# A hybrid decoder trunk on TensorE: gate on 80 partitions, paired levels, a diagonal on VectorE

## What is computed

```python
def rmsnorm(x, g):
    return x * rsqrt(mean(x * x, axis=-1) + EPS) * g

def hybrid_mixer(h, cos, sin, w_in, w_a2, b_a2, ret_norm_g, gla_norm_g, w_out):   # h = rmsnorm(x, mix_pre_g)
    rq, rk, rv, rg, gq, gk, gv, ga, gg = split(h @ w_in)     # ga has 16 columns, gq and gk 256 each
    ro = retention(rope(rq), rope(rk) * 64 ** -0.5, rv)      # chunks of 128 tokens, 4 heads
    ro = rmsnorm(ro, ret_norm_g) * silu(rg)
    log_a = log_sigmoid(ga @ w_a2 + b_a2) / 16               # 16 -> 256, per key dimension
    go = gla(gq * 64 ** -0.5, gk, gv, log_a)                 # gated linear attention, 4 heads
    go = rmsnorm(go, gla_norm_g) * silu(gg)
    return concat(ro, go) @ w_out

# gla, unchunked: S_t = diag(exp(log_a_t)) S_{t-1} + k_t^T v_t ;  o_t = q_t S_t
# so the score of query i on key j <= i is sum_d q_id k_jd exp(cum_id - cum_jd), cum the running sum of log_a;
# for i = j the exponent is 0 and the score is q_i . k_i
```

## Time and profile before

| | us |
|---|---|
| median of 3 runs | 1191.17 (1190.92 to 1191.26) |
| profiled execution | 1191.56 |
| its span, first to last instruction | 1189.8 |
| TensorE busy | 1182.7 |
| VectorE busy | 831.0 |
| ScalarE busy | 703.1 |
| GpSimd busy | 147.7 |

### The profile page before, as it was taken

How to read it: one execution, slowest core, us unless ns; L and a number is a source line. 1 busy time by engine, 2 the same in 40 slices (tenths; PEclk the granted TensorE clock), 3 DMA queues, 4 the chain that set the end, 5 groups by cost and what they waited for, 6 DMA issues and landing times. The chain is left out here.

```text
span 1189.8 us, 17467 instructions
## 1 busy us (share of the span) xinstructions
PE 1182.7 (99%) x6224; PEld 1001.9 (84%) x6224; DVE 831.0 (70%) x1290; ACT 703.1 (59%) x1223; POOL 147.7 (12%) x230
## 2 busy tenths in 40 slices
PE   9999999999999999999999999999999999999998
PEld 8888888778888888888888888887888888888886
DVE  6866546788767678775487875477887676777752
ACT  7655446756666557654476664376566665666641
POOL 3000002473100100000000000026531001000000
PEclk9999999999999999999999999999999999999999
DMA  9755555354545365556465555554445444555540
GB/s 366 258 183 195 198 207 185 136 213 142 168 169 177 116 209 191 193 195 211 142 213 199 189 198 191 194 207 136 171 142 183 153 163 155 191 202 180 196 173 36
DMA packets 33350, 217.81 MB, mean 183 GB/s; under 512 B 3953, under 2 KB 4209, under 8 KB 9729
## 3 DMA queue, kind: packets, MB, share of 16 engines
q1 hardware_dynamic: 33136, 216.77, 52.6%
q10 hardware_dynamic: 144, 0.13, 0.0%
HBM read 215.84 MB, written 1.05 MB: 182 GB/s over the span
## 5 line engine op out<-in xcount | busy, mean ns | idle before, releaser
L1539 DVE SCALAR_TENSOR_TENSOR w_lo<-raw,first,w_hi 128x512 fp32r<-128x512 f32 x576 | 414.7, 774 | 87.9 <-ACT w_hi L1084 87.4
L1084 ACT ACTIVATE w_hi<-raw,first 128x512 fp32r<-128x512 f32 x568 | 368.7, 715 | 98.9 <-PE acc L756 47.5
L755 PE MATMUL acc<-xT,w_hi 128*128 128x512 f32 x864 | 300.2, 391 | 0.0
L756 PE MATMUL acc<-xT,w_lo 128*128 128x256 f32 x864 | 241.9, 280 | 0.0
L580 PE MATMUL acc<-w_hi,xT 128*128 128x512 f32 x576 | 228.7, 397 | 0.0
L581 PE MATMUL acc<-w_hi,xT 128*128 128x512 f32 x576 | 224.6, 390 | 0.0
L584 PE MATMUL acc<-w_lo,xT 128*128 128x512 f32 x576 | 224.4, 390 | 0.0
L755 PEld LDWEIGHTS acc<-xT,w_hi 128*128 128x128 f32 x864 | 161.6, 187 | 35.4
L1531 DVE TENSOR_TENSOR w_lo<-raw,w_hi 128x1024 fp32r<-128x1024 f32 x112 | 124.6, 1146 | 89.9 <-ACT w_hi L1078 89.6
L756 PEld LDWEIGHTS acc<-xT,w_lo 128*128 128x128 f32 x864 | 163.3, 189 | 0.1
L1078 ACT ACTIVATE w_hi<-raw 128x1024 fp32r<-128x1024 f32 x112 | 106.6, 991 | 95.3 <-PE acc L584 78.7
(11 more groups left out here) (224 smaller groups left out, 1382.7 us busy)
## 6 DMA issues: line engine op xcount, KB each, us to landing
raw<-in_gu SPq DMA_DIRECT2D x86, 1024.0 KB, 5.1
raw<-in_down SPq DMA_DIRECT2D x32, 1024.0 KB, 4.8
raw<-in_in SPq DMA_DIRECT2D x24, 1024.0 KB, 5.1
raw<-in_kv SPq DMA_DIRECT2D x16, 1024.0 KB, 5.1
raw<-in_down SPq DMA_DIRECT2D x16, 768.0 KB, 4.2
raw<-in_out SPq DMA_DIRECT2D x8, 1024.0 KB, 5.1
raw<-in_q SPq DMA_DIRECT2D x8, 1024.0 KB, 5.1
raw<-in_o SPq DMA_DIRECT2D x8, 1024.0 KB, 5.0
```

What stands on the lines that cost most here:

```text
L755: pe.matmul(o[:, :], w_hi[:, slot, kk, c:c + P], xT[:, :, k, :], start=k == 0, stop=False)
L756: mm = pe.matmul(o[:, TOK:2 * TOK], w_lo[:, slot, kk, c:c + P], xT_hi[:, k, :], start=False, stop=k == KD - 1)
L1084: act.activation(w_hi[:, slot, k, :], raw[:, slot, k, :], ACT.Copy, scale=gains[:, ds(g, 1)]).then_inc(s_hi, 1)
L1539: dve.scalar_tensor_tensor(w_lo[:, slot, k, :], raw[:, slot, k, :], gains[:, ds(g, 1)], w_hi[:, slot, k, :].bitcast(F32), ALU.mult, ALU.su ...
```

## The change

The mixer's input is normalised before it is transposed, as for the FFNs. The low-rank gate's weights stand five times side by side in 80 columns (hi, lo, hi, hi, hi), so that ga comes out on 80 partitions, and 16 matmuls (all 80 columns times xT_hi, then times xT_lo) replace 24. VectorE rounds the 80 rows to fp32r and puts the remainder into rows 32 to 47; w_a2 stands on the same 80 partitions (three times, zeros, once more, of which its low part is kept), so that one fp32r product per half gives the logits. The diagonal comes from VectorE: query times key, row sums, times the identity. Two levels share one use of the banks, each with its half (`LV_USE`, `LV_HALF`); the second retention keys share with level 0. The squares of `mem` and its 1/rms move into the down chunks of the first FFN.

```diff
-M_USES = ["z", "diag", "rj0", "rj1", "lv0", ..., "lv7", "ro", "go", "s0", "s1"]
+M_USES = ["z", "rj0", "rj1lv0", "lv1", "lv23", "lv45", "lv67", "ro", "go", "s0", "s1"]
+LV_USE = ["rj1lv0", "lv1", "lv23", "lv23", "lv45", "lv45", "lv67", "lv67"]
+LV_HALF = [1, 0, 0, 1, 0, 1, 0, 1]
 # SyncE: mem is loaded in layer 0's first FFN, mem_t behind the mixer's last x transposes
+                if (l, f) == (0, 0):
+                    sp.wait_ge(s_tev, 4)
+                    sp.dma_start(mem_t[:, :, :], a["mem"].rearrange("(t p) d -> p t d", p=P)).then_inc(s_mem, 16)
-                        sp.wait_ge(s_x, l * 16 + 8)
+                        sp.wait_ge(s_t, t_no(l, ("x", 1, 1, 1)) + 1)
-                            sp.wait_ge(s_msq, 2)
 # TensorE
-                norm = phase in (0, 3, 4)
+                norm = phase != 2
+                    if d == 3 and (l, f) == (0, 0):
+                        pe.wait_ge(s_rmem, TT)
+                        for i in range(TT):
+                            mm = pe.matmul(mb[0][:, i * P:(i + 1) * P], r_mem[:, i:i + 1].to_broadcast([P, P]),
+                                           ident[:, :], start=True, stop=True)
-                late = (dict(before_last=lambda: x_transposes(l, 1, 0)) if f == 0 else
-                        dict(mids={3: lambda: x_transposes(l, phase + 1, 0)}))
+                     ..., mids={3: lambda: x_transposes(l, phase + 1, 0)})
                     for kt in range(KD):
-                        three(mb[0][0:RANK, 0:TOK], w_ga_hi[:, kt, :], w_ga_lo[:, kt, :], xT_hi[:, kt, :],
-                              xT_lo[:, kt, :], kt == 0, kt == KD - 1)
-                    pe.wait_ge(s_rpre, l * 8 + 2 + 1 + 1)
-                    for t in range(TT):
-                        mm = pe.matmul(mb[0][0:RANK, TOK + t * P:TOK + (t + 1) * P],
-                                       r_pre[:, t:t + 1].to_broadcast([P, RANK]), ident[:, :], start=True, stop=True)
+                        st = w_ga_cols[:, kt, :, :].rearrange("p c r -> p (c r)")
+                        pe.matmul(mb[0][0:GA_COLS, 0:TOK], st, xT_hi[:, kt, :], start=kt == 0, stop=False)
+                        mm = pe.matmul(mb[0][0:GA_COLS, 0:TOK], st, xT_lo[:, kt, :], start=False, stop=kt == KD - 1)
-                inside = {4: {4: diagonal}, 5: {4: lambda: retention_scores(0)}, 6: {4: lambda: level(l, 0)}, ...
+                def second_keys():
+                    retention_scores(1)
+                    level(l, 0, False, True)
+                inside = {5: {4: lambda: retention_scores(0)},
+                          6: {4: lambda: level(l, 1, True, True)}, 10: {4: retention_outputs}}
+                behind = {4: rqk_transposes, 5: second_keys, 6: lambda: levels(l, 2), 7: lambda: levels(l, 4),
+                          8: lambda: levels(l, 6), 10: gated_outputs, 11: lambda: mixed_transposes(l, 0)}
 # ScalarE, start of the mixer (boundary() now has the FFNs' order too)
+                x_square(l, 1, 1)
                 act.wait_ge(s_gas, l + 1)
-                act.activation(w_ga_hi[:, :, :], w_ga_s[:, :, :], ACT.Copy).then_inc(s_gah, 1)
+                act.activation(w_ga_cols[:, :, :, :], w_ga_s[:, :, :].unsqueeze(2).to_broadcast([P, KD, 5, RANK]),
+                               ACT.Copy).then_inc(s_gah, 1)
+                act.activation(w_a2_l[:, :], w_a2[:, l, :], ACT.Copy).then_inc(s_a2hi, 1)
                 split_hi(l, C_IN + 1, 1)
                 x_hi(l, 1, 1)
-                x_square(l, 1, 1)
-                act.wait_ge(s_rpre, l * 8 + 2 + 0 + 1)
-                project(0, 0, gqk[:, 0, :], r_pre)
+                project(0, 0, gqk[:, 0, :], 1.0)
 # VectorE
+                x_norm(l, 1, 1)
                 dve.tensor_tensor(w_ga_s[:, :, :], ..., g_mix, ALU.mult).then_inc(s_gas, 1)
                 split_lo(l, C_IN + 1, 1)
                 x_lo(l, 1, 1)
-                dve.tensor_copy(r_row, mb[0][0:RANK, TOK:2 * TOK]).then_inc(s_rrow, 1)
-                dve.tensor_tensor(gaT, mb[0][0:RANK, 0:TOK], r_row, ALU.mult).then_inc(s_mf[0], 1)
+                dve.tensor_copy(gaT[:, :], mb[0][0:GA_COLS, 0:TOK]).then_inc(s_gahi, 1)
+                low = slice(2 * RANK, 3 * RANK)
+                dve.tensor_tensor(gaT[low, :], mb[0][low, 0:TOK], gaT[low, :].bitcast(F32),
+                                  ALU.subtract).then_inc(s_mf[0], 1)
+                dve.tensor_tensor(qk, gqk[:, :, 0:256], gqk[:, :, 256:512], ALU.mult).then_inc(s_qk, 1)
+                dve.tensor_reduce(qk_dot[:, :], pr0[:, 0]..., AX.X, ALU.add).then_inc(s_qk, 1)
                 for e in range(2):
-                    dve.tensor_tensor(pg[:, e], mb[e][:, :].rearrange("p (c i) -> p c i", c=4),
-                                      ident[:, :].unsqueeze(1).to_broadcast([P, 4, P]), ALU.mult).then_inc(s_mf[e], 1)
+                    dve.tensor_tensor(pg[:, e], ident[:, :].unsqueeze(1).to_broadcast([P, 4, P]), d,
+                                      ALU.mult).then_inc(s_pg, 1)
                 retention_mask(1)
-                split_lo(l, C_IN + 4, 0, ks=(0, 1))
                 level_out(0)
-                split_lo(l, C_IN + 4, 0, ks=(2, 3))
-                split_lo(l, C_IN + 4, 1, ks=(0, 1))
+                split_lo(l, C_IN + 4, 0)
                 level_out(1)
```

More of the change, by code:

```diff
@@ L807, in level @@
                 A = av[n % 2].rearrange("p (r i) -> p r i", r=2)
-                for e in range(2):
-                    wait_m(l, f"lv{n}", e)
-                if l == 0 and n == 6:
-                    pe.wait_ge(s_rmem, TT)
-                    for t in range(TT):
-                        pe.matmul(mb[0][:, TOK + t * P:TOK + (t + 1) * P], r_mem[:, t:t + 1].to_broadcast([P, P]),
-                                  ident[:, :], start=True, stop=True)
+                c0 = LV_HALF[n] * TOK
+                if first:
+                    for e in range(2):
+                        wait_m(l, LV_USE[n], e)
                 if b == P:
@@ L819, in level @@
                             rows = slice(64 * e, 64 * e + 64)
[L820 removed]
+                            mm = pe.matmul(mb[e][:, c0 + r * P:c0 + (r + 1) * P], A[rows, r, 0:P], A[rows, r, P:2 * P],
                                            start=True, stop=True)
[L822 removed]
+                            if last and r == 1:
                                 mm.then_inc(s_m[e], 1)
@@ L2246, in _ @@
                     pool.wait_ge(s_const, 16 * 5)
+                    for t in range(TT):
+                        mem_norm(l, t)
                 post(l, 0, 0)
```

231 lines of the change are left out of this document (113 added, 118 removed).

## The result

The changed kernel takes 1193.77 us (median of 15 runs, 1193.32 to 1194.88), the kernel before 1191.17 beside it: 1.0021 times as long, 95% interval 1.0014 to 1.0028. The forecast was 1188.4, and the time lies above its range. The profiled execution took 1193.32 us, 1.76 more than that of before.

The account below looks back on a forecast made before the run. TensorE, busy 1182.7 of 1189.8 us, was taken as the bound. Program −8.8, boundary +4.9 and middle +1.2 make −2.7: 1188.9 us profiled, 1188.4 to 1188.5 as median; forecast's own range 1186.2 to 1190.2, 8 in 10 1184.4 to 1191.4.

Parts of the forecast that it names:

- The program taken from TensorE: Mixer: low-rank gate, logits, diagonal and switches shorten TensorE's program by 4.5 us per layer.
- The low-rank block with the pass behind it: Low-rank gate in the mixer: 16 matmuls replace 24 and the row of 1/rms goes, gain 1.6 us per layer.
- the logits: Gate logits in the mixer: two fp32r products replace true FP32, gain 0.8 us per layer.
- the switches: Mixer passes broken by FP32 blocks: four breaks fewer at 0.23 us each, gain 0.9 us per layer.
- The boundary: Start of the mixer: TensorE waits 2.45 us per layer ahead of tile 1's first pass, 4.9 in both layers.
- The middle of the mixer: Log gate through levels: TensorE waits for VectorE 0.6 us per layer, 1.2 in all, bounds 0 and 1.5 per layer.
- The added work: VectorE's product and row sums, each about 0.64 us, fit the 2.1 us in which it waited for the log gate.
- one of the same size: VectorE in the mixer's middle: the diagonal's write replaces a write of equal size, so adds nothing.
- one wait of 0.4 and one of 0.2: TensorE waits 0.4 us at the first retention scores and 0.2 us for level 1's bank, per layer.
- The shared port: Diagonal's write contends with GpSimd's first exponents in SBUF: 1.2 us worse over both layers, not in the sum.
- The gain is eaten in the middle: Rival: the middle's waits cost 4.2 us instead of 1.2, time 1191.4, no change; chance 0.20.
- The clock rival: Rival: waits at each mixer's start drop TensorE's clock, 2.8 us per stretch, 5.6 in all, time 1194.0; chance 0.08.

Follow-up runs that it names:

- e11: e9 with the levels unpaired (one use of the banks each) and VectorE's and ScalarE's orders of the kernel before in the middle; 1188.25 us.
- e1: Changed kernel with ScalarE's gate-weight copies, and the wait ahead of them, moved behind the split and the copies of tile 1's transposes; 1190.17 us.
- e9: Changed kernel with the diagonal back on TensorE and the ScalarE edit of e1; 1187.42 us.
- e15: e10 without tile 1's rotary and with GpSimd's first exponents behind the diagonal's write, result not the reference's; 1183.03 us.
- e10: e1 with GpSimd's level exponents and products cut to one column, the first two exponents a whole plain copy; 1185.67 us.
- e17: Changed kernel with six matmuls that nobody reads ahead of TensorE's wait for rT; 1193.96 us.
- e7: Changed kernel with the diagonal back on TensorE and VectorE's product and row sums removed; 1191.13 us.
- e16: e4 with six matmuls that nobody reads ahead of TensorE's wait for the first mask; 1188.65 us.
- e12: e9 with the transposed retention queries and keys (rT) copied out of PSUM by ScalarE instead of VectorE; 1187.58 us.
- e2: Changed kernel with VectorE reordered: rT copy ahead of the diagonal's write, first mask and the level's copies ahead of a split; 1192.79 us.
- e4: Changed kernel with both ScalarE's move of e1 and VectorE's order of e2; 1189.71 us.
- e6: e5 with the product of query and key and its row sums moved ahead of the logits' bias; 1192.54 us.
- e13: e4 with 14 matmuls that nobody reads ahead of TensorE's wait for the first mask; 1190.72 us.
- e5: e1 with the rT copy ahead of the diagonal's write, the first mask behind one low part, other splits spread behind it; 1190.71 us.

## Why the prediction was wrong

- **The program taken from TensorE** (4.5 us per layer) was right and undersized: 5.2 to 5.5. The low-rank block with the pass behind it gave 1.8 us where 1.6 was forecast, the logits 0.8 as forecast. The term that was too small is the switches: a removed pass break is worth 0.37 us, not 0.23 (e11).
- **The boundary** (2.45 per layer) was right: the first pass of tile 1 came at T + 14.55 and T + 14.25 where T + 14.25 follows from the forecast's wait, and the ledger gives 2.90 and 2.62. Of it 1.8 is ScalarE's queue behind the gate weights (e1); the rest, late transposes of the normalised tile and their low parts, is still there in e9.
- **The step that failed is "The middle of the mixer"**, taken at 0.6 us per layer, at most 1.5. It measured 3.6 in layer 0 and 3.3 in layer 1. The added work did fit into the 2.1 us in which VectorE waited for the log gate, as forecast (0.31 were left). What failed is the price of VectorE's instructions at their new places beside GpSimd. First, the chain was expected 0.8 us earlier with its old lengths, so the copy of rT done at E + 10.93. It was done at E + 11.97: the log-gate step took 1.50 us instead of 0.69, beside the rotary; the diagonal's write, "one of the same size", took 1.69 instead of 1.26, beside the first exponents (alone 1.27, e15); two low parts gave 0.18 back. TensorE came at E + 10.37, with 10.55 expected, and waited 1.66. Second, level 1's copy was done at E + 26.0 (246.23), not E + 23.2. The split just ahead of it had been taken at 4.00 and took 4.17, nearly right. The lateness is the 1.04 us from above and the low parts around the first mask, 2.30 instead of 1.76 and 4.56 instead of 3.62 (four of them took 2.72 alone, e10). So the queue did not stop at one wait of 0.4 and one of 0.2: in layer 0 waits of 1.18 and 0.72 us followed. TensorE had also become 3.4 to 3.7 us quicker through this stretch, and VectorE, which had kept pace beside the slower program, had to follow.
- **The shared port.** The rule had been weighed at +1.2 us and left out of the sum, though the 4.00 us of a split beside GpSimd was in it. By the Trainium skill, "SBUF — State Buffer", "Who interferes with whom", a VectorE instruction with two SBUF inputs contends with GpSimd's reads. The runs agree, and with a larger price: GpSimd's levels cost 4.5 us of the kernel's time (e10 against e1), and its rotary of one tile, with its first exponents beside the diagonal's write, 2.6 more (e15 against e10).
- **The rivals.** "The gain is eaten in the middle" was the right mechanism, with a bound still too small (4.2 us in both layers against 6.8). The clock rival gave nearly the right time, 1194.0, by luck: in the profiled execution the lower level came once, behind a wait in the middle and at neither boundary, lost 1.6 us where 2.8 had been put down for each mixer, and cost nothing on top of the waits (e17).
- What it would have taken: the added work was compared with an engine's idle time before the change. What counts is the idle time left in the shorter stretch, up to each point where TensorE waits. In the changed kernel VectorE is busy 29.18 of the first 30 us from E, before 25.35; over the whole way to ro it is 45.82 of 51.55 against 42.56 of 52.00, and the idle time left there lies behind the waits.

What stays open: why one wait of 1.65 us was followed by the lower clock and its twin was not, and how much of the boundary's remaining 0.8 to 1.1 us per layer could be had; no run took it on.

## What to carry to other kernels

Before work is moved off the bounding engine, add up the receiving engine's work over the stretch as it will be, shortened by what is saved and with each instruction at its price beside the engine that it shares a port with; if that is close to full, the move can lose more than it saves (here 1.23 us of matmuls per layer were taken away, and the kernel is 1.3 us per layer slower than with them left in, e7). Changing the order of a full engine's work moved the wait each time and won little: at most 0.5 us by the medians and 1.5 with the clock kept up (e16), where taking GpSimd's work away from beside it won 4.5 (e10). A copy that waits for its own input does not belong ahead of a conversion that the bounding engine needs next. The version with the low-rank gate on 80 partitions and the paired levels, but the diagonal on TensorE and ScalarE's copies late (e9), is faster than both kernels, 1187.42 us.

## What the runs showed of the hardware

- VectorE beside GpSimd, against alone: product of two SBUF tiles 1.18 against 0.68 us, log-gate step 1.50 against 0.69 (1.03 to 1.05 where it met less of the rotary, e7 to e9 and e12), the diagonal's two writes 1.69 (up to 2.31 in the runs with the copy of rT ahead of them, e2, e4 to e6, e13 and e16) against 1.27, four low parts up to 4.56 against 2.72. Instructions with an operand in PSUM kept their lengths: copies of rT and first masks 1.27 to 1.29 each, and the diagonal's write with the matmuls' result as one operand 1.26 beside the same exponents (before, e7, e9). It goes both ways: beside the product the rotary's second step took 1.90 against 1.45.
- A single stop of TensorE in a dense stretch can be followed by the lower clock, and its length alone does not decide it. In the profiled executions a stretch at 0.50 stood behind waits of 1.65 us (changed kernel, layer 1), 1.83 (e2), 1.83 and 1.82 (e4), 1.69 and 1.66 (e5), 1.90 and 2.44 (e6), and 0.87 (e2 and e13, layer 1). It did not come behind 1.66 (changed kernel, layer 0), 1.82 (e2, layer 1), 1.63 twice (e1), 1.5 twice (e10), nor behind 0.87 in e13's layer 0 and twice in e16. The Trainium skill's "TensorE: Matmul & The Clock Gate", "HAM oscillation — how this bites in real kernels", tells of idle stretches between bursts of matmuls; in these traces one short stop was enough in ten places.
- Putting an FP32 block between the fp32r matmuls of a pass costs more than the block: 0.37 us per break, as two single levels with their pass take 7.97 us where a pair takes 7.60 (e11, e9).
